# First projection: the second weight chunk is loaded, split and multiplied behind the second modulation pair

## The reference, cut to what matters

```python
c_act = jax.nn.silu(c)
mod = c_act @ w_ada + b_ada            # (1024) @ (1024 x 6144)
sh1, sc1, ga1, sh2, sc2, ga2 = split(mod, 6)
h = rmsnorm(x, g_attn) * (1.0 + sc1) + sh1
proj = h @ w_in                        # (512 x 1024) @ (1024 x 2632), the first projection
```

## Time and profile before

| | |
|---|---|
| median of 3 runs | 1025.82 us (1025.13 to 1025.96) |
| the profiled execution | 1027.5 us, of which the span of instructions is 1025.7 us |
| TensorE busy in matmuls | 1008.7 us, 98% of the span |
| VectorE, ScalarE, GpSimd busy | 783.2, 520.4, 506.3 us |
| mean granted TensorE clock | 0.997 of full speed |
| DMA | 129.01 MB, mean 126 GB/s |

### The profile page before, as it was taken

How to read it: one execution, slowest core, us unless ns; L and a number is a source line. 1 busy time by engine, 2 the same in 40 slices (tenths; PEclk the granted TensorE clock), 3 DMA queues, 4 the chain that set the end, 5 groups by cost and what they waited for, 6 DMA issues and landing times.

```text
span 1025.7 us, 16087 instructions
## 1 busy us (share of the span) xinstructions
PE 1008.7 (98%) x5886; PEld 847.1 (83%) x5886; DVE 783.2 (76%) x1473; ACT 520.4 (51%) x808; POOL 506.3 (49%) x210
## 2 busy tenths in 40 slices
PE   6999999999999999999999999999999999999997
PEld 5687788667888999999978888888887778888887
DVE  6358998786876555655687875699999999988975
ACT  4243324885267556556562223525526888363263
POOL 0024243673345865665544434347865676634350
PEclk9999999999999999999999999999999999999999
DMA  9985222150213333243289752234231222322312
GB/s 323 349 286 161 83 83 82 43 165 2 82 53 112 102 125 102 87 138 103 83 276 318 252 179 83 83 112 134 83 122 42 83 82 94 112 83 86 120 42 83
DMA packets 127387, 129.01 MB, mean 126 GB/s; under 512 B 3680, under 2 KB 125408, under 8 KB 127328
## 3 DMA queue, kind: packets, MB, share of 16 engines
q1 hardware_dynamic: 126080, 127.38, 38.5%
q10 hardware_dynamic: 1248, 0.86, 0.3%
HBM read 126.13 MB, written 2.10 MB: 125 GB/s over the span
## 4 chain that ended last, share of the span: by engine, by line
PE 75%; issue 11%; POOL 9%; DMA 1%; ACT 1%; SPq 1%; POOLq 0%; DVE 0%; ACTq 0%; DVEq 0%
PE bank L857 16%; PE bank L859 16%; PE bank L858 15%; POOL w_a L779 3%; POOL w_hi L779 2%; PE bank L1200 2%; PE bank L1171 2%; PE bank L1043 2%; POOL w_s L788 2%; POOL w_lo L686 2%; PE bank L1492 1%; PE bank L1494 1%; PE bank L1493 1%; PE bank L869 1%; PE bank L870 1%
## 5 line engine op out<-in xcount | busy, mean ns | idle before, releaser
L686 POOL TENSOR_TENSOR w_lo<-w_stage,w_hi 128x2048 fp32r<-128x2048 f32 x56 | 269.1, 4805 | 357.8 <-ACT w_hi L1606 346.9
L857 PE MATMUL bank<-act_hi,w_hi 128*128 128x512 f32 x496 | 197.4, 398 | 0.1
L859 PE MATMUL bank<-act_hi,w_lo 128*128 128x512 f32 x496 | 193.2, 389 | 0.0
L858 PE MATMUL bank<-act_lo,w_hi 128*128 128x512 f32 x496 | 193.1, 389 | 0.0
L1606 ACT ACTIVATE w_hi<-w_stage 128x2048 fp32r<-128x2048 f32 x57 | 109.1, 1913 | 122.1 <-PE bank L859 105.1
L2873 DVE SCALAR_TENSOR_TENSOR bank<-v_pad,vcol,bank 128x512 f32<-128x512 f32 x208 | 138.2, 745 | 0.0
L857 PEld LDWEIGHTS bank<-act_hi,w_hi 128*128 128x128 f32 x496 | 93.1, 188 | 24.9 <-issue 4.9
L858 PEld LDWEIGHTS bank<-act_lo,w_hi 128*128 128x128 f32 x496 | 93.2, 188 | 20.1 <-issue 1.4
L859 PEld LDWEIGHTS bank<-act_hi,w_lo 128*128 128x128 f32 x496 | 93.1, 188 | 19.8
L857 PE MATMUL bank<-ff_hi,w_hi 128*128 128x512 f32 x176 | 69.9, 397 | 1.2 <-POOL w_lo L686 1.2
L859 PE MATMUL bank<-ff_hi,w_lo 128*128 128x512 f32 x176 | 69.3, 394 | 0.0
(11 more groups left out here) (463 smaller groups left out, 2698.1 us busy)
## 6 DMA issues: line engine op xcount, KB each, us to landing
w_stage<-in_w_in SPq DMA_DIRECT2D x29, 1024.0 KB, 5.2
ada_stage<-in_w_ada SPq DMA_DIRECT2D x20, 1024.0 KB, 11.6
w_stage<-in_w_gu SPq DMA_DIRECT2D x14, 1024.0 KB, 5.1
w_stage<-in_w_out SPq DMA_DIRECT2D x12, 1024.0 KB, 5.1
late_stage<-in_mod_w SPq DMA_DIRECT2D x12, 1024.0 KB, 9.1
w_stage<-in_w_gu SPq DMA_DIRECT2D x16, 512.0 KB, 3.6
w_stage<-in_w_down SPq DMA_DIRECT2D x8, 1024.0 KB, 5.5
late_stage<-in_w_ada SPq DMA_DIRECT2D x4, 1024.0 KB, 10.7
```

What stands on the lines that cost most here:

```text
L686: nc.gpsimd.tensor_tensor(low[:], w_stage[b][:], high[:].bitcast(F32), ALU.subtract).then_inc(s_lo, 1)
L857: pe.matmul(dst, wh, rhs_hi(k), start=(first and k == 0), stop=False)
L858: pe.matmul(dst, wh, rhs_lo(k), start=False, stop=False)
L859: mm = pe.matmul(dst, wl, rhs_hi(k), start=False, stop=(last and k == n_k - 1))
```

## The change

SyncE issues the load of weight chunk 1 behind the two modulation chunks of pair 1 and no longer ahead of them. TensorE does slices 2 and 3 of chunk 0's tiles directly behind pair 1's modulation, and only then waits for chunk 1's low part and does slices 0 and 1 of chunk 1's tiles. ScalarE and VectorE make the parts of chunk 1 behind pair 1's slices, where they had made them behind pair 0's. No instruction is added or taken away.

```diff
             first_chunk_dma(0)
-            w_in_dma(1)
             ada_dma(ADA_PE[2])
             ada_dma(ADA_PE[3])
+            w_in_dma(1)
             first_chunk_dma(1)
...
                     pe.wait_ge(s_lo0, 1)
                     abreast(first, 0, (0, 1))
                     ada_pair(1)
+                    abreast(first, 0, (2, 3))
                     pe.wait_ge(s_lo0, 2)
                     abreast(second, 0, (0, 1))
-                    abreast(first, 0, (2, 3))
                     ada_pair(2)
...
-                if j == 0:
+                if j == 1:
                     act.wait_ge(s_stage[1], 16)
                     nc.scalar.activation(w_hi[1][:], w_stage[1][:], ACT.Copy).then_inc(s_hi0, 1)
-                elif j == 1:
                     hi_half(1)
...
-                if j == 0:
+                if j == 1:
                     dve.wait_ge(s_hi0, 2)
                     V.tensor_tensor(w_lo[1][:], w_stage[1][:], w_hi[1][:].bitcast(F32), ALU.subtract).then_inc(s_lo0, 1)
```

## The result

| | before | after |
|---|---|---|
| median | 1025.49 us (6 runs, 1025.13 to 1025.96) | 1029.28 us (6 runs, 1028.57 to 1030.12) |
| ratio after / before | | 1.0036, 95% interval 1.0025 to 1.0047 |
| profiled execution | 1027.5 us | 1028.83 us |
| its span | 1025.7 us | 1027.0 us |

The change makes the kernel 3.8 us slower (1029.28 - 1025.49). From profile to profile the end moved by 1.3 us only. The first puzzle is therefore that the profiles show a third of what the timed runs show.

What follows compares the result with a forecast made beforehand. TensorE, busy 98% of the span, was taken to bound the kernel; pair 1's 1.26 us gain is outweighed by an uncovered path and low clock, net +1.85 on 1025.82, giving 1027.7 us, range 1026.4 to 1029.4.

Steps and rivals of the forecast that it cites:

- Pair 1's gain: Pair 1 on TensorE: both modulation chunks land in time, so VectorE's first instruction on the result comes 1.26 us earlier.
- rival B: Load queue: loads share and don't queue, so pair 1's gain is missing; +2.8 to +3.8 us, around 1028.9; chance 0.05.
- What is late next: TensorE after pair 1: idle from about 28.6 to 31.6 us, since nothing covers VectorE's and ScalarE's path to slice 2.
- floor: Earliest start of pair 2's rows, set by chunk 1's low part at 35.42: 38.55 us, +1.51.
- measuring point: Start of pair 2's modulation rows on TensorE, 37.04 us before; behind it both kernels have the same order.
- The clock: TensorE's low clock on slices 2 and 3 after the idle stretch: +1.85 us, between +1.5 and +2.5.
- What is moved past: ScalarE's `hi_half(1)`, GpSimd's low half and SyncE's loads of chunks 2 and 3 (1.9 us later): costs nothing, DMA engines don't run dry.
- C: Later on TensorE: a 1.2 us wait for GpSimd's low part swallows up to 1.2 of the delay; around 1026.4; chance 0.10.
- D: Faster: the VectorE and ScalarE path is covered and the low clock goes too; -2.9 us, 1022.9; chance 0.03.
- The sum: Whole kernel: the added 1.85 us carried over to the median shown, 1025.82 + 1.85 = 1027.7 us.
- Rival A: Timed runs of before lack the profile's low clock, so the change costs +3.1 to +4.1 us, around 1029.2; chance 0.24.
- the likeliest case: The forecast itself with its bounds of +1.5 to +2.5 us, own range 1027.3 to 1028.3; chance 0.58.

Runs made afterwards that it cites:

- e1: Changed kernel plus 11 warming products (result unused) in TensorE's idle stretch before slices 2 and 3; 1028.62 us, 1.0029 to before.
- e4: Changed kernel with ScalarE's split of chunk 1 moved ahead of pair 1's high parts; 1029.70 us, 1.0039 to before.
- e2: Kernel before with 4 warming products in TensorE's 1.07 us wait between the rows of pair 1's two chunks; 1025.95 us, 1.0002 to before.
- e0: Kernel before, unchanged, run and profiled once more; 1025.77 us, 1.0000 to before.

## Why the prediction was right, and what was off

*Pair 1's gain.* Expected VectorE's first instruction at 28.71; it is at 28.62, 1.35 us earlier than before. The rows of pair 1 needed no wait for a load, so the landing moved as the order of the loads said, and rival B is out.

*What is late next.* Expected the idle stretch to end at 31.59 and chunk 1's low part at 35.42; measured 31.41 and 33.03 + 2.29 = 35.32. The floor of the measuring point was 38.55; e1, at full clock, has 38.33.

*The clock.* Expected +1.85 by a low stretch as long as before, between bounds of +1.5 and +2.5. The profile has +1.65, e4 shows the upper bound. The Trainium skill's rule that bursts of matmuls with longer waits between them run the next burst throttled ("TensorE: Matmul & The Clock Gate", "HAM oscillation — how this bites in real kernels") spoke against the change. The trace of after agrees in that the clock fell about when the 2.83 us wait ended (0.97 from 30 to 32 us, 0.50 from 32 to 34), and each execution of after has a mean clock of 0.998 or less. The delay was nearer the lower bound, where by that rule it would have been at the upper one.

*What is moved past.* The second wait of the loads' queue was seen (37.92 and not 36.05), but one sentence of this step was wrong: the DMA engines did run dry, with 189 GB/s between 38 and 40 us where there had been 343. It cost nothing, as the constant 1.6 us to the last matmul shows. The same constant rules out C: the wait that was to swallow part of the delay (line 857 for GpSimd's low part, 1.2 us before) is there after as well, with 1.1 us. D is out by the sign of the result.

*The sum: the step that failed.* "The median shown is 1.7 lower than that execution; carried over, 1025.82 + 1.85". The 1.7 is not an overhead that both kernels have. Most of it is the 3.4 us of low clock that the profile of before contains and 54 of 60 executions, by their mean clocks, do not. After has it always, so the timed difference is the profile's 1.65 plus those 1.6 (by e2: 1.42), 3.1 to 3.3, and 0.5 to 0.7 remain. After's median lies 0.45 above its profiled execution, and two of its executions have the longer stretch (0.996); but its slowest, 1030.12, is at 0.998, so the remainder is not explained by the clock alone and stays open. The mechanism was right, and the base of the sum was not. Rival A said this, with 1029.2 us and a chance of 0.24, and its for-argument, that the 1.7 of distance and the 1.6 of price agree, was the better evidence. It deserved to be the forecast. That the time lies in the range owes something to luck: the likeliest case's own range (1027.3 to 1028.3) missed it, the upper bound of 1029.4 came from giving A a part, and three of the six executions lie above that bound. A's two ends, 1025.82 + 3.1 and + 4.1, give 1028.9 to 1029.9, so 1029.4 is the middle of A and not of its upper half, as the prediction has it. It had also named "if the end moves by another amount than the measuring point" as a sign of being wrong. From profile to profile both moved alike (1.62 and 1.65); against the timed 3.8 us the sign was there, and it pointed at the base.

## What to carry to other kernels

Before adding a difference to the median, ask whether the profiled execution is a typical one. If it lies above all timed runs by just what a low-clock stretch in it costs, the stretch may be missing in the others; the mean clock of each execution tells. A wait of 1 us on TensorE is cheap compared with 12 matmuls taken away from under a path of 3 us over two other engines: look at what a block covers before moving it. And where a load delays something more urgent, move only the half of it that isn't needed yet.

## What was not expected of the hardware

Whether the clock falls varies between executions of the same program: before had a mean of 0.997 in 6 of 60 and 0.999 to 1.000 in the others, and the six take about 1.1 to 1.7 us more than the median (1026.66 to 1027.25 against about 1025.5). In both profiles of that kind the fall follows a stretch in which TensorE did only the small modulation matmuls and turns and waited for about 1.1 us (1.07 and 1.18) for a load; with that wait filled (e2) it came in none of 11. Both profiles of before that were taken, here and in e0, were of the rare kind; with two profiles it stays open whether that is chance.
